# A decoder block on one core: group loads behind the fourth weight load of a group, and row fetches spread evenly

## The chip, the cores and the metric

The kernel runs on one core of a Trainium2 chip. The metric is device time in microseconds (us), shorter is better. TensorE multiplies, VectorE (DVE) and ScalarE (ACT) work elementwise, GpSimd (POOL) does elementwise work and issues indirect DMAs, and SyncE (SP) only issues DMAs.

## The reference

One hybrid decoder block for 512 tokens of width 2048 in float32: a gated mixer (an mLSTM branch and an RWKV-7 branch), then PEER, a retrieval of single-neuron experts, then an RMSNorm. The change lies in PEER:

```python
q = (xt @ w_query).reshape(NT, PEER_HEADS, 2, D_KEY // 2)
s = einsum('nhpd,pkd->nhpk', q, sub_keys)
...  # top 16 of 16 x 16 sums per head: idx [token, 128], gate = softmax(best)
act = gelu(einsum('cd,ced->ce', xc, expert_u[ic]))
out = einsum('ce,ced->cd', gc * act, expert_v[ic])
```

There are 128 x 128 = 16384 experts, each with a row of 2048 in `expert_u` and in `expert_v`; each token uses 8 heads x 16 = 128 of them.

## The kernel before, in words

PEER is done in two ways side by side. For the first 128 tokens (G) the expert rows themselves are fetched: 128 fetches of u rows, each an indirect DMA of GpSimd that brings one row of 2048 for each of the 128 tokens (1.05 MB), and then 128 fetches of v rows. VectorE uses each: a u row is multiplied with the token and summed into `dots` (line 1416), a v row is scaled by `coef` and added to a sum that lies in four PSUM banks (line 1419). Between the two halves stands one change: ScalarE's gelu of `dots`, VectorE's `coef` (lines 1462 to 1465). For the other 384 tokens (N) all experts are computed densely: 128 score units give gelu(x u) of 128 experts each, stored in `gelu_scratch`; the gates are laid out densely in `gates_scratch`; and 32 groups of 4 x 128 experts, in 4 units each (`pe_values`), multiply gate times gelu with all v rows.

All weights come through one stream of 396 units of 128 x 2048 floats (1.05 MB). SP loads unit n into `raw[n % 2]` once GpSimd has finished with unit n - 2 (`load_unit`, line 333); ScalarE copies it to a high part `wh` once TensorE has used unit n - 2 (`split_hi`, line 339); GpSimd subtracts for a low part `wl` (`split_lo`, line 343); TensorE does 48 matmuls, three for each of 16 blocks. A value group needs 1.5 MB besides: its gates `gt` and activations `act` (`load_group`, lines 514 and 515), on SP's queue among the weight loads. GpSimd multiplies them (`gated`, line 629), ScalarE makes the high half `gah`, VectorE the residual `gal` (line 1423), all one group ahead; TensorE waits for the last residual of a group before its first unit. Buffers of two groups alternate, so pass g of the loop sends group g + 2 once the residuals of group g are made (`gal_ready`). The very first pass also sends group 1, at its third load, and waits for all of `gelu_scratch` to be stored before it sends group 2.

GpSimd's program is: split of a unit, then the row fetches that stand behind it in a list, then `gated`. The list has two parts: `REST_FETCHES` for the last 40 score units (r = 0 to 39, the first fetch at r = 2) and `VALUE_FETCHES` for the 128 value units (k = 0 to 127). Before, there are two fetches behind each unit until the u rows end at k = 27, none at k = 28 to 30, and 2, 1, 2, 1, ... v rows from k = 31 to 115. A fetch waits until VectorE has used the row that had its buffer (`row_used`); there are three buffers (`ROWS_REST`) in the score part and five from two fetches into the value part. VectorE uses the rows behind unit k - 1 between its additions of unit k, after the second and the third (`dve_values`). The first u row can't be used before TensorE has transposed the 128 tokens (`xd`), which stands behind the fourth of these 40 score units.

Of the kernel before, what the change touches and what calls it, by code (L numbers as in the profile page):

```python
# [57 lines left out]
SLOTS = HEADS * TOPK  # L58
# [5 lines left out]
GROUPS = NKEYS // GE  # L64
NC4 = D // T
N_UNITS = U_PEER + NC4 * GROUPS


F_REST = NKEYS - SC_REST
REST_FETCHES = [range(2 * r - 4, 2 * r - 2) if 2 <= r < F_REST - 2 else range(0) for r in range(F_REST)]  # L70
N_REST = REST_FETCHES[F_REST - 3][-1] + 1
V_FIRST = 31
VALUE_FETCHES = [range(min(N_REST + 2 * k, SLOTS), min(N_REST + 2 * k + 2, SLOTS)) for k in range(V_FIRST)]
for k in range(V_FIRST, NC4 * GROUPS):
    at = SLOTS + 3 * ((k - V_FIRST) // 2) + 2 * ((k - V_FIRST) % 2)
    VALUE_FETCHES.append(range(min(at, 2 * SLOTS), min(at + 2 - (k - V_FIRST) % 2, 2 * SLOTS)))
assert not VALUE_FETCHES[NC4 * 7] and not VALUE_FETCHES[NC4 * 29 + 1]

ROWS_REST, ROWS = 3, 5
ROW_AT = [n % ROWS_REST if n < N_REST + 2 else n % ROWS for n in range(2 * SLOTS)]  # L80
# [3 lines left out]

R_GATED = F_REST - 5


def score_unit(e):
    return U_QUERY + PER_HEAD * (e // SC_HEAD) + 2 + e % SC_HEAD if e < SC_HEAD * HEADS else U_ROUTED + e - SC_HEAD * HEADS
# [47 lines left out]
def build(nc, stream, lora_w, params, x_t, keys_t, u_rows, v_rows, out_t):  # L137
# [13 lines left out]
    with ctx:  # L151
# [178 lines left out]
        def load_unit(sp, n, s, first=False):  # L330
            if not first:
                sp.wait_ge(w_lo, n - 1)
            sp.dma_start(raw[s][:, :], stream[bass.ds(n, 1)].rearrange("a p n -> p (a n)")).then_inc(w_loaded[s], 16)
# [7 lines left out]
        def split_lo(pool, n, s):  # L341
            pool.wait_ge(w_hi, n + 1)
            pool.tensor_tensor(wl[s][:, :], raw[s][:, :], wh[s][:, :].bitcast(F32), ALU.subtract).then_inc(w_lo, 1)  # L343
# [101 lines left out]
        def _(sp):  # L445
# [66 lines left out]
            def load_group(g, s):  # L512

                sp.dma_start(gt[s][:, :, :], gate_d[:, :, bass.ds(GE * g, GE), :].rearrange("b p e t -> p b (e t)")).then_inc(group_in[s], 16)
                sp.dma_start(act_[s][:, :, :], act_d[bass.ds(GE * g, GE)].rearrange("e p t -> p e t")).then_inc(group_in[s], 16)
# [8 lines left out]
            def load_values(g, s, ahead=True, first=False):  # L524

                for c in range(NC4):
                    load_unit(sp, U_PEER + NC4 * g + c, c % 2)
                    if c == 1 and ahead:
                        for r in range(2):
                            sp.wait_ge(pre_stored[r], 16 + 8 * NKEYS)  # L530
                        sp.wait_ge(gal_ready, GE * g + GE)
                        load_group(g + 2, s)
                    if c == 2 and first:
                        sp.wait_ge(w_used, U_PEER)
                        load_group(1, 1)

            for s in range(2):
                load_values(s, s, first=s == 0)
            with sp.Fori(1, GROUPS // 2 - 1) as i:
                for s in range(2):  # L540
                    load_values(2 * i + s, s)
            for s in range(2):
                load_values(GROUPS - 2 + s, s, ahead=False)
# [7 lines left out]
        def _(pool):  # L551
# [68 lines left out]
            def fetch(n):  # L620
                if ROW_LAST[n] is not None:
                    pool.wait_ge(row_used, ROW_LAST[n] + 1)
                pool.indirect_dma_start(rowb[ROW_AT[n]][:, :], None, u_rows if n < SLOTS else v_rows,  # L623
                                        bass.IndirectOffsetOnAxis(ap=idx[:, n % SLOTS:n % SLOTS + 1], axis=0)).then_inc(row_in[ROW_AT[n]], 16)
# [6 lines left out]

            for r in range(F_REST):
                split_lo(pool, score_unit(SC_REST) + r, r % 2)
                if r == 2:
                    pool.wait_ge(slots_ready, 1)
                    for s in range(2):
                        pool.wait_ge(gates_stored[s], 16 + 8 * GB)
                for n in REST_FETCHES[r]:
                    fetch(n)
# [4 lines left out]
            for k in range(NC4 * GROUPS):  # L644
                g, c = divmod(k, NC4)
                split_lo(pool, U_PEER + k, c % 2)
                if k == 1:
                    pool.wait_ge(w_used, U_PEER)
                for n in VALUE_FETCHES[k]:
                    fetch(n)  # L650
# [9 lines left out]
        def _(act):  # L660
# [336 lines left out]
            def act_halves(g, s, e):  # L997
                act.wait_ge(ga_ready, GE * g + e + 1)
                act.activation(gah[s][:, e, :], act_[s][:, e, :], ACT.Copy).then_inc(gah_ready, 1)  # L999

            def rest(e, s):
                act_ahead(e, s, score_unit(SC_REST) + e - SC_REST)
# [4 lines left out]
            for e in range(GE):  # L1007
                act_halves(0, 0, e)
            for r in range(R_GATED + 1, F_REST):
                rest(SC_REST + r, r % 2)  # L1010

            def act_values(g, s, ahead=AHEAD):
                for c in range(NC4):
                    n = U_PEER + NC4 * g + c
                    for e in ahead[c]:
                        act_halves(g + 1, 1 - s, e)
                    act.wait_ge(w_used, n + 1)
                    split_hi(act, n + 2, c % 2)

            for s in range(2):  # L1020
                act_values(s, s, AHEAD_1 if s == 0 else AHEAD)
            with act.Fori(1, 4) as i:
                for s in range(2):
                    act_values(2 * i + s, s)
            act.wait_ge(row_used, SLOTS)
            act.activation(gel[:, :], dots[:, :], ACT.Gelu).then_inc(gel_ready, 1)
            with act.Fori(4, GROUPS // 2 - 1) as i:
                for s in range(2):
                    act_values(2 * i + s, s)
            act.wait_ge(row_used, 2 * SLOTS)  # L1030
# [5 lines left out]
            g = GROUPS - 1  # L1036
# [22 lines left out]
        def _(dve):  # L1059
# [213 lines left out]
            at = slice(2 * MH - 2, 2 * MH)  # L1273
            dve.wait_ge(ymh_ready, 1)
            dve.tensor_tensor(yl_m[:, at, :], ymo[:, :, :], yh_m[:, at, :].bitcast(F32), ALU.subtract).then_inc(yml_ready, 1)
            for h in range(MH - 1):
                at = slice(2 * h, 2 * h + 2)
# [133 lines left out]
            def use(n):  # L1411

                b = rowb[ROW_AT[n]][:, :]
                dve.wait_ge(row_in[ROW_AT[n]], 16 * ROW_BEFORE[n] + 16)
                if n < SLOTS:
                    dve.scalar_tensor_tensor(b, b, 1.0, xg, ALU.mult, ALU.mult, accum_out=dots[:, n:n + 1]).then_inc(row_used, 1)  # L1416
                else:
                    dve.wait_ge(row_used, n)
                    dve.scalar_tensor_tensor(xg, b, coef[:, n - SLOTS:n - SLOTS + 1], xg, ALU.mult, ALU.add).then_inc(row_used, 1)  # L1419

            def dve_low(g, s, e):
                dve.wait_ge(gah_ready, GE * g + e + 1)
                dve.tensor_tensor(gal[s][:, e, :], act_[s][:, e, :], gah[s][:, e, :].bitcast(F32), ALU.subtract).then_inc(gal_ready, 1)  # L1423

            def dve_rows(g, c, dd):

                n = U_PEER + NC4 * g + c
                if dd == 3:
                    dve.wait_ge(w_used, n + 1)
                else:  # L1430
                    dve.wait_ge(out_ready, 3 * (NC4 * g + c) + dd + 1)
                at = H[:, 4 * c + dd, G:T]
                dve.tensor_tensor(at, bank(4 + dd)[:, 0:N], at, ALU.add).then_inc(out_added, 1)  # L1433

            def dve_values(g):

                for c in range(NC4):
                    k = NC4 * g + c
                    fetched = list(VALUE_FETCHES[k - 1]) if k else []
                    dve_rows(g, c, 0)  # L1440
                    dve_rows(g, c, 1)
                    for n in fetched[:1]:
                        use(n)
                    dve_rows(g, c, 2)
                    for n in fetched[1:]:
                        use(n)
                    for e in (AHEAD if g else AHEAD_1)[c]:
                        dve_low(g + 1, 1 - g % 2, e)
                    dve_rows(g, c, 3)
# [3 lines left out]
            dve.wait_ge(xg_ready, 1)  # L1453
            for r in range(F_REST):
                for n in REST_FETCHES[r]:
                    use(n)
                if r == R_GATED:
                    for e in range(GE):
                        dve_low(0, 0, e)
            for g in range(8):  # L1460
                dve_values(g)
            dve.wait_ge(row_used, SLOTS)
            dve.memset(xg, 0.0)
            dve.wait_ge(gel_ready, 1)
            step(dve.tensor_tensor(coef[:, :], gel[:, :], gate0[:, :], ALU.mult))
            for g in range(8, GROUPS - 1):
                dve_values(g)


            for b in range(4):  # L1470
                dve.wait_ge(sum_out, b + 1)
                at = H[:, 4 * b:4 * b + 4, 0:G]
# [8 lines left out]
            g = GROUPS - 1  # L1481
# [495 lines left out]
```

## Time and profile before

| | |
|---|---|
| Median of 3 runs (4293.15, 4306.17, 4307.22) | 4306.17 us |
| The profiled execution | 4302.8 us, of it span 4301.0 |
| Busy: TensorE, weight load, VectorE, ScalarE, GpSimd | 97, 87, 60, 30, 53% of the span |
| One split of a unit: ScalarE, GpSimd | 1.9, 4.6 us (means 1917, 4644 ns) |
| One load of a group, on SP | 768 KB of gates and 768 KB of activations |
| DMA over the span | 832.09 MB, 193 GB/s |
| Mean granted TensorE clock | 0.985 |

The span has three parts that matter here: score units with row fetches from about 2794 us, value units from 3138 to 4278 us, and in these the change from u to v rows near 3460 us. The DMA share is the mean busy share of the core's 16 DMA engines.

### The profile page before, as it was taken

What the parts mean: (1) busy time and instruction counts of PE and PEld (TensorE: products, weight loads), DVE (VectorE), ACT (ScalarE), POOL (GpSimd) and SP (SyncE); (2) the same over time, 40 slices, a digit from 0 to 9 for tenths busy, and PEclk for the clock granted to TensorE, in tenths of its full rate; (3) what the DMA queues carried; (4) which work ended last, traced back from release to release, by engine and by line L of the source; (5) the groups of instructions that cost most, each with busy time, mean ns of one, the idle gap of its engine ahead of it and who ended that gap; (6) DMA issues with size and microseconds to landing.
All of it is one profiled execution on the core that took longest, in us unless ns stands there. A gap on an engine that the chain in (4) does not pass through costs nothing.

```text
span 4301.0 us, 69877 instructions
## 1 busy us (share of the span) xinstructions
PE 4162.1 (97%) x27220; PEld 3743.0 (87%) x27220; DVE 2571.1 (60%) x3908; ACT 1306.7 (30%) x1265; POOL 2259.6 (53%) x866
## 2 busy tenths in 40 slices
PE   7999999999999999899999999999988999999998
PEld 5777777777788778799999999999978999999997
DVE  4344343444554542477775999745558777777775
ACT  4332322333322221233233444422222222222223
POOL 4333223233234344344445544567767778888884
PEclk9999999999999999999999999999999999999999
DMA  3222222222223442233334555499979989899983
GB/s 121 89 88 80 86 87 82 84 87 87 97 89 104 140 170 98 80 122 122 123 120 145 191 188 195 186 353 395 380 291 356 356 326 356 351 358 360 357 329 109
DMA packets 205230, 832.09 MB, mean 193 GB/s; under 512 B 15864, under 2 KB 98040, under 8 KB 120080
## 3 DMA queue, kind: packets, MB, share of 16 engines
q1 hardware_dynamic: 135024, 486.69, 31.5%
q0 software_dynamic: 36864, 268.45, 15.1%
q10 hardware_dynamic: 33184, 74.63, 4.5%
q8 instruction: 125, 2.05, 0.2%
q14 instruction: 33, 0.27, 0.0%
HBM read 760.99 MB, written 68.71 MB: 193 GB/s over the span
## 4 chain that ended last, share of the span: by engine, by line
PE 79%; issue 9%; POOL 4%; DVE 3%; DMA 3%; ACT 1%; SPq 0%; POOLq 0%; DVEq 0%; ACTq 0%
PE ps L348 17%; PE ps L350 16%; PE ps L349 16%; PE ps L1874 7%; PE ps L1875 7%; PE ps L1876 7%; POOL wl L343 4%; DMA raw<-stream 2%; PE ps L1578 2%; PE ps L1836 1%; ACT wh L339 1%; DVE rowb L1416 1%; DVE gal L1423 1%; PE ps L1730 0%; PE ps L1721 0%
## 5 line engine op out<-in xcount | busy, mean ns | idle before, releaser
L343 POOL TENSOR_TENSOR wl<-raw,wh 128x2048 fp32r<-128x2048 f32 x396 | 1839.0, 4644 | 1878.5 <-ACT wh L339 1878.0
L348 PE MATMUL ps<-xh,wh 128*128 128x384 f32 (+1 forms) x3904 | 1463.3, 375 | 43.4 <-POOL wl L343 22.2
L350 PE MATMUL ps<-xh,wl 128*128 128x384 f32 (+1 forms) x3904 | 1430.0, 366 | 0.0
L349 PE MATMUL ps<-xl,wh 128*128 128x384 f32 (+1 forms) x3904 | 1429.4, 366 | 0.0
L339 ACT ACTIVATE wh<-raw 128x2048 fp32r<-128x2048 f32 x396 | 759.0, 1917 | 1937.5 <-PE ps L350 1066.2
L348 PEld LDWEIGHTS ps<-xh,wh 128*128 128x128 f32 x3904 | 737.9, 189 | 140.4 <-issue 36.8
L350 PEld LDWEIGHTS ps<-xh,wl 128*128 128x128 f32 x3904 | 737.4, 189 | 83.4
L349 PEld LDWEIGHTS ps<-xl,wh 128*128 128x128 f32 x3904 | 738.1, 189 | 81.3 <-issue 7.7
L1874 PE MATMUL ps<-gah,wh 128*128 128x384 f32 x2048 | 699.7, 342 | 44.4 <-POOL wl L343 22.3
L1875 PE MATMUL ps<-gal,wh 128*128 128x384 f32 x2048 | 696.7, 340 | 0.0
L1876 PE MATMUL ps<-gah,wl 128*128 128x384 f32 x2048 | 696.1, 340 | 0.0
L1433 DVE TENSOR_TENSOR H<-ps,H 128x384 f32<-128x384 f32 x512 | 277.8, 553 | 320.3 <-PE ps L1876 317.5
L1874 PEld LDWEIGHTS ps<-gah,wh 128*128 128x128 f32 x2048 | 388.5, 190 | 49.5 <-issue 18.8
L1875 PEld LDWEIGHTS ps<-gal,wh 128*128 128x128 f32 x2048 | 388.7, 190 | 0.0
L1876 PEld LDWEIGHTS ps<-gah,wl 128*128 128x128 f32 x2048 | 388.5, 190 | 0.0
L1416 DVE SCALAR_TENSOR_TENSOR rowb<-rowb,ps 128x2048 f32<-128x2048 f32 x128 | 291.9, 2282 | 161.1 <-DMA rowb<-u_rows,idx 137.3
L1419 DVE SCALAR_TENSOR_TENSOR ps<-rowb,coef,ps 128x2048 f32<-128x2048 f32 x128 | 300.3, 2346 | 0.0
L623 POOL DMA_INDIRECT rowb<-u_rows,idx x128 | 123.4, 964 | 91.1 <-DVE rowb L1416 73.7
L1379 DVE TENSOR_SCALAR oh<-ps,EGT,gate_l 128x128 fp32r<-128x128 f32 x384 | 154.7, 403 | 0.0
L1379 DVE TENSOR_SCALAR oh<-ps,EGT,gate_h 128x128 fp32r<-128x128 f32 x384 | 154.7, 403 | 0.0
L1423 DVE TENSOR_TENSOR gal<-act,gah 128x384 fp32r<-128x384 f32 x128 | 150.5, 1197 | 1.4 <-ACT gah L999 1.4
L623 POOL DMA_INDIRECT rowb<-v_rows,idx x128 | 126.5, 988 | 25.7 <-issue 17.1
(321 smaller groups left out, 3700.6 us busy)
## 6 DMA issues: line engine op xcount, KB each, us to landing
raw<-stream SPq DMA_DIRECT2D x396, 1024.0 KB, 4.8
gelu_scratch<-preb ACTq DMA_DIRECT2D x128, 192.0 KB
gates_scratch<-stage ACTq DMA_DIRECT2D x12, 2048.0 KB, 6.5
gt<-gates_scratch SPq DMA_DIRECT2D x32, 768.0 KB
act<-gelu_scratch SPq DMA_DIRECT2D x32, 768.0 KB
mergegate_scratch<-sgb ACTq DMA_DIRECT2D x32, 256.0 KB, 2.1
sgm<-mergegate_scratch SPq DMA_DIRECT2D x32, 256.0 KB, 2.7
h_in<-x_t SPq DMA_DIRECT2D x4, 1024.0 KB, 8.8
```

The lines of the kernel that those rows point to most:

```text
L339: act.activation(wh[s][:, :], raw[s][:, :], ACT.Copy).then_inc(w_hi, 1)
L343: pool.tensor_tensor(wl[s][:, :], raw[s][:, :], wh[s][:, :].bitcast(F32), ALU.subtract).then_inc(w_lo, 1)
L348: pe.matmul(dst, w_h, h[:, kx, lo:], start=start, stop=False)
L349: pe.matmul(dst, w_h, l[:, kx, lo:], start=False, stop=False)
L350: return pe.matmul(dst, w_l, h[:, kx, lo:], start=False, stop=stop)
L1379: last = dve.tensor_scalar(oh1[:, 4 * c + u, m, :], iota_ps, EGT[:, 0, bass.ds(at + u, 1)], gate[:, bass.ds(at + u, 1)], ALU.is_equal, ALU ...
L1416: dve.scalar_tensor_tensor(b, b, 1.0, xg, ALU.mult, ALU.mult, accum_out=dots[:, n:n + 1]).then_inc(row_used, 1)
L1419: dve.scalar_tensor_tensor(xg, b, coef[:, n - SLOTS:n - SLOTS + 1], xg, ALU.mult, ALU.add).then_inc(row_used, 1)
L1433: dve.tensor_tensor(at, bank(4 + dd)[:, 0:N], at, ALU.add).then_inc(out_added, 1)
L1874: pe.matmul(dst, w_h, gah[s][:, e, :], start=e == 0, stop=False)
L1875: pe.matmul(dst, w_h, gal[s][:, e, :], start=False, stop=False)
L1876: last = pe.matmul(dst, w_l, gah[s][:, e, :], start=False, stop=e == GE - 1)
```

## The change

The wait for the residuals and the load of group g + 2 stand behind the fourth weight load of pass g and no longer behind the second. The row fetches are spread by rounding: 128 u rows over 74 units (r = 2 to 37 and k = 0 to 37), 128 v rows over 78 units (k = 39 to 116). The change from u to v rows, on ScalarE and VectorE, stands in front of group 10 and no longer of group 8.

```diff
+V_GROUP = 10
+U_UNITS, V_UNITS = F_REST - 4 + NC4 * V_GROUP - 2, NC4 * 29 - (NC4 * V_GROUP - 1) + 1
+even = lambda i, units: range(SLOTS * i // units, SLOTS * (i + 1) // units)
-REST_FETCHES = [range(2 * r - 4, 2 * r - 2) if 2 <= r < F_REST - 2 else range(0) for r in range(F_REST)]
+REST_FETCHES = [even(r - 2, U_UNITS) if 2 <= r < F_REST - 2 else range(0) for r in range(F_REST)]
 N_REST = REST_FETCHES[F_REST - 3][-1] + 1
-V_FIRST = 31
-VALUE_FETCHES = [range(min(N_REST + 2 * k, SLOTS), min(N_REST + 2 * k + 2, SLOTS)) for k in range(V_FIRST)]
-for k in range(V_FIRST, NC4 * GROUPS):
-    at = SLOTS + 3 * ((k - V_FIRST) // 2) + 2 * ((k - V_FIRST) % 2)
-    VALUE_FETCHES.append(range(min(at, 2 * SLOTS), min(at + 2 - (k - V_FIRST) % 2, 2 * SLOTS)))
+VALUE_FETCHES = []
+for k in range(NC4 * GROUPS):
+    i = k - (NC4 * V_GROUP - 1)
+    n = even(i, V_UNITS) if 0 <= i < V_UNITS else range(0)
+    VALUE_FETCHES.append(even(F_REST - 4 + k, U_UNITS) if k < NC4 * V_GROUP - 2 else range(SLOTS + n.start, SLOTS + n.stop))
...
                     load_unit(sp, U_PEER + NC4 * g + c, c % 2)
-                    if c == 1 and ahead:
+                    if c == 3 and ahead:
                         for r in range(2):
                             sp.wait_ge(pre_stored[r], 16 + 8 * NKEYS)
                         sp.wait_ge(gal_ready, GE * g + GE)
...
-            with act.Fori(1, 4) as i:
+            with act.Fori(1, V_GROUP // 2) as i:
...
-            with act.Fori(4, GROUPS // 2 - 1) as i:
+            with act.Fori(V_GROUP // 2, GROUPS // 2 - 1) as i:
...
-            for g in range(8):
+            for g in range(V_GROUP):
                 dve_values(g)
...
-            for g in range(8, GROUPS - 1):
+            for g in range(V_GROUP, GROUPS - 1):
                 dve_values(g)
```

The counts that result: r = 2 to 37 get 1, 2, 2, 1, 2, 2, 2, 1, ... (62 u rows in 36 units, 72 before); k = 0 to 37 get 66 u rows (2, 1, 2, 2, 1, 2, 2, 2, 1, ...); k = 38 none; k = 39 to 116 get 1, 2, 1, 2, 2, 1, 2, 2, ... v rows. The three row buffers last until fetch 63 and the five start at fetch 64 (73 and 74 before).

## Rows read from the trace of the kernel before

**Rows 1.** Sums by stretch: length, busy us (instructions) per engine, clock, DMA share, GB/s

```profile
2794.00:2833.00 39.00, 30.86 (x169) 30.58 (x168) 12.20 (x11) 6.89 (x7) 21.90 (x12) 0.87 0.74 278
2833.00:3034.00 201.00, 201.00 (x1144) 201.00 (x1144) 107.73 (x95) 55.05 (x48) 154.49 (x71) 1.00 0.99 393
3034.00:3138.00 104.00, 96.56 (x537) 95.53 (x535) 51.05 (x44) 29.17 (x28) 73.92 (x36) 0.98 0.87 340
3138.00:3206.00 68.00, 49.97 (x250) 49.02 (x251) 39.15 (x40) 9.93 (x10) 39.10 (x22) 0.85 0.86 322
3206.00:3443.00 237.00, 217.28 (x1195) 214.84 (x1195) 197.56 (x224) 59.88 (x52) 183.48 (x95) 0.97 0.88 347
3443.00:3498.00 55.00, 51.59 (x285) 51.27 (x285) 38.14 (x37) 13.58 (x12) 40.86 (x20) 0.97 0.77 298
3498.00:4242.00 744.00, 743.77 (x4228) 742.98 (x4227) 531.42 (x562) 207.31 (x180) 615.15 (x295) 1.00 0.87 337
```

**Rows 2.** DMA issues of the page: count, KB each, median us to landing

```profile
raw<-stream SPq DMA_DIRECT2D x396, 1024.0 KB, 4.8
```

**Rows 3.** Timeline beside a v group: start us, us, engine and operation, idle before

```profile
3551.21 4.63 POOL L343 TENSOR_TENSOR wl<-raw,wh 128x2048 fp32r<-128x2048 f32 x1 [0.20 <-ACT wh L339]
...
3559.53 0.38 SPq L514 DMA_DIRECT2D gt<-gates_scratch  x1
...
3575.45 1.92 ACT L339 ACTIVATE wh<-raw 128x2048 fp32r<-128x2048 f32 x1 [7.00 <-DMA raw<-stream]
```

**Rows 4.** Timeline beside a u group: GpSimd's split, ScalarE's split two units later

```profile
3371.95 4.63 POOL L343 TENSOR_TENSOR wl<-raw,wh 128x2048 fp32r<-128x2048 f32 x1
...
3400.37 1.92 ACT L339 ACTIVATE wh<-raw 128x2048 fp32r<-128x2048 f32 x1 [11.97 <-DMA raw<-stream]
```

**Rows 5.** Timeline of ScalarE, VectorE and GpSimd where row fetches begin

```profile
2803.63 1.92 ACT L339 ACTIVATE wh<-raw 128x2048 fp32r<-128x2048 f32 x1 [6.17 <-PE ps L350]
...
2813.67 2.29 DVE L1416 SCALAR_TENSOR_TENSOR rowb<-rowb,ps 128x2048 f32<-128x2048 f32 x1 [23.57 <-PE ps L1855]
...
2816.24 0.94 POOL L623 DMA_INDIRECT rowb<-u_rows,idx  x1 [13.33 <-DVE rowb L1416]
2817.19 4.52 POOL L343 TENSOR_TENSOR wl<-raw,wh 128x2048 fp32r<-128x2048 f32 x1
```

**Rows 6.** Timeline: load of group 0 and ScalarE's split of the load behind it

```profile
3034.74 0.39 SPq L514 DMA_DIRECT2D gt<-gates_scratch  x1
...
3058.50 1.92 ACT L339 ACTIVATE wh<-raw 128x2048 fp32r<-128x2048 f32 x1 [12.02 <-DMA raw<-stream]
```

**Rows 7.** Sums of a stretch behind a stall, columns as in rows 1

```profile
3250.20:3257.00 6.80, 5.19 (x16) 5.20 (x17) 3.38 (x4) 2.40 (x2) 6.33 (x5) 0.50 0.60 225
```

**Rows 8.** Timeline of the first value units: GpSimd, SP, ScalarE, VectorE

```profile
3129.36 4.62 POOL L343 TENSOR_TENSOR wl<-raw,wh 128x2048 fp32r<-128x2048 f32 x1 [3.82 <-ACT wh L339]
...
3146.25 2.37 SPq L333 DMA_DIRECT2D raw<-stream  x1
...
3156.39 1.91 ACT L339 ACTIVATE wh<-raw 128x2048 fp32r<-128x2048 f32 x1 [18.28 <-DMA raw<-stream]
...
3175.20 6.57 DVE L1423 TENSOR_TENSOR gal<-act,gah 128x384 fp32r<-128x384 f32 x2
```

**Rows 9.** Waits from 3134 to 3206 us: in total, times, longest us

```profile
PE ps L1874 <- DVE gal L1423: 8.3, 1, 8.3
...
PE ps L1874 <- POOL wl L343: 7.5, 1, 7.5
```

**Rows 10.** SP's waits for residuals, 3206 to 3443 us, then 3498 to 4242 us

```profile
SPq L514 <- DVE gal L1423: 24.5, 6, 10.4
...
SPq L514 <- DVE gal L1423: 56.8, 20, 3.1
```

**Rows 11.** Costliest groups of the page: busy us, mean ns of one, idle before

```profile
L1416 DVE SCALAR_TENSOR_TENSOR rowb<-rowb,ps 128x2048 f32<-128x2048 f32 x128 | 291.9, 2282 | 161.1 <-DMA rowb<-u_rows,idx 137.3
```

**Rows 12.** Timeline of VectorE at the change from u to v rows

```profile
3462.21 4.25 DVE L1465 TENSOR_TENSOR coef<-gel,gate 128x128 f32<-128x128 f32 x1
```

More of the change, by code:

```diff
@@ L69 @@
 F_REST = NKEYS - SC_REST
-REST_FETCHES = [range(2 * r - 4, 2 * r - 2) if 2 <= r < F_REST - 2 else range(0) for r in range(F_REST)]
+V_GROUP = 10
+U_UNITS, V_UNITS = F_REST - 4 + NC4 * V_GROUP - 2, NC4 * 29 - (NC4 * V_GROUP - 1) + 1
+even = lambda i, units: range(SLOTS * i // units, SLOTS * (i + 1) // units)
+REST_FETCHES = [even(r - 2, U_UNITS) if 2 <= r < F_REST - 2 else range(0) for r in range(F_REST)]
 N_REST = REST_FETCHES[F_REST - 3][-1] + 1
-V_FIRST = 31
-VALUE_FETCHES = [range(min(N_REST + 2 * k, SLOTS), min(N_REST + 2 * k + 2, SLOTS)) for k in range(V_FIRST)]
-for k in range(V_FIRST, NC4 * GROUPS):
-    at = SLOTS + 3 * ((k - V_FIRST) // 2) + 2 * ((k - V_FIRST) % 2)
-    VALUE_FETCHES.append(range(min(at, 2 * SLOTS), min(at + 2 - (k - V_FIRST) % 2, 2 * SLOTS)))
-assert not VALUE_FETCHES[NC4 * 7] and not VALUE_FETCHES[NC4 * 29 + 1]
+VALUE_FETCHES = []
[3 more added lines that the diff above has]
+    VALUE_FETCHES.append(even(F_REST - 4 + k, U_UNITS) if k < NC4 * V_GROUP - 2 else range(SLOTS + n.start, SLOTS + n.stop))
+assert sum(map(len, REST_FETCHES + VALUE_FETCHES)) == 2 * SLOTS and not VALUE_FETCHES[NC4 * 29 + 1]
 ROWS_REST, ROWS = 3, 5
```

## The prediction

> **What bounds the kernel now.** I read the per-stretch sums first [rows 1]. TensorE is the bound wherever nothing stands in its way: in the stretch 3498 to 4242 us it did 4228 matmuls in 744.0 us, 5.68 per us, so a unit of 48 matmuls takes 8.44 us. With 5.69 per us as the full rate, each stretch's loss is its length less its matmuls over 5.69:
> - 2794 to 2833 (first row fetches): 39.0 - 169/5.69 = 9.3 us
> - 2833 to 3034 (score units with two fetches each): 201.0 - 1144/5.69 = 0
> - 3034 to 3138: 104.0 - 537/5.69 = 9.6
> - 3138 to 3206 (first value units): 68.0 - 250/5.69 = 24.1
> - 3206 to 3443 (rest of the u rows): 237.0 - 1195/5.69 = 27.0
> - 3443 to 3498 (change to v rows): 55.0 - 285/5.69 = 4.9
> - 3498 to 4242 (v rows): 744.0 - 4228/5.69 = 0.9
>
> Together 75.8 us, all that a new order of transfers and rows can win. Where TensorE did not lose, the DMA is nearly full: 393 GB/s at share 0.99, with no matmul lost. So saturation alone costs nothing; what costs is a weight transfer that stands behind a group's 1.5 MB. In the 201 us stretch weight transfers (1.05 MB) land in about 4.8 us, the page's median [rows 2], in spite of two rows of 1.05 MB each.
>
> **The deadline of a weight transfer.** Call t = 0 the end of the low split of unit n-2, when SP may send the load of unit n. ScalarE splits unit n when TensorE ends unit n-2, 10.2 us later in steady state; the two splits (1.9 and 4.6 us) end 1.4 us before TensorE needs them. A load issued right behind a group therefore follows 8.4 us after the preceding one, and must have landed 8.4 + 10.2 + 1.4 = 20.0 us after the split that let the preceding one go. In a v group [rows 3] that split ended at 3551.21 + 4.63 = 3555.84, the group went at 3559.53 and its follower landed at 3575.45: 19.6 us, 0.4 to spare. In the seventh u group [rows 4] the split ended at 3371.95 + 4.63 = 3376.58, landing 3400.37: 23.8 us, 3.8 late. Between them lie three bursts of rows (2, 1, 2) against (2, 2, 2); one more row of 1.05 MB at 393 GB/s is 2.7 us.
>
> **Part 1, a later start of the rows.** Before, fetches 2 and 3 follow the third split of that stage; row 3 needs row 0's buffer, and row 0 can't be used before TensorE has transposed xd, behind the unit that precedes. GpSimd stands for 13.33 us in front of the fetch and its split starts at 2817.19 though ScalarE's half began at 2803.63 and took 1.9 [rows 5]. With the even spread the counts for r = 2, 3, 4 are 1, 2, 2: row 3 comes one split later, so the split at 2817.19 goes back to about 2805.5 and TensorE runs that unit straight after the transposes, at 2813.5. Then GpSimd waits for rows 0 and 1 (done at 2815.9 and 2818.1), its next split ends at 2819.3 + 4.6 = 2823.9, and TensorE, free at 2821.9, waits 2.0 us. Loss 9.3 becomes 2.0: -7.3. Bounds: 0 (the stall moves on whole) to -9.3.
>
> **Part 2, group 0.** It goes at 3034.74, and its follower lands at 3058.50 [rows 6], 23.8 us behind it where the v group's came 15.9 behind and had 0.4 to spare. TensorE's stall of some 4.5 us and the half clock behind it are 6.0 of the 9.6 lost. The clock's part: after such a stall the granted clock was 0.50 (1.2 GHz of 2.4), and 5.19 us of busy TensorE held 16 matmuls, worth 2.8 at the full rate: 2.4 us for the longest, 1.5 for shorter ones [rows 7]. In the new plan score units carry 62/36 = 1.72 rows, (1.72 + 1) x 1.05 + 0.20 for the gelu store = 3.05 MB in 8.44 us, 361 GB/s instead of 396, and the bursts there are (2, 2, 1). I take 2 us late, no half clock: -4 (0 to -6).
>
> **Part 3, the first value groups.** SP stands behind the last gelu store before it sends group 2, and the raw load of value unit 2 behind it goes only at 3146.25, 12.3 us after its buffer was free; ScalarE gets it at 3156.39 [rows 8]. Behind the fourth load, group 2 no longer blocks units 2 and 3; group 1 goes at once after load 2. Unit 2 then lands by 3140 and costs nothing (TensorE waits 7.5 us for it before). Next in line is the residual of group 1, for which TensorE waits 8.3 us [rows 9]. It came late because two of VectorE's subtractions took 6.57 us [rows 8] where GpSimd's split lay beside them. New: rows 64 to 66 are taken in bursts 1, 2, 2; row 65 shares its buffer with row 63 across the change from three to five buffers, so GpSimd stands some 3 us once. I get the split of unit 3 at 3160.8 to 3165.4, the last residual of group 1 at 3176, against 3172 wanted: 4 us late, 1 for the clock. Loss 24.1 becomes 5: -19. Bounds: -5 (the residuals are as late as before) to -22.
>
> **Part 4, u groups.** Value units carry 66/38 = 1.74 u rows instead of 2: 3.26 MB a unit, 387 GB/s for 419. 419 can't be had, 387 just can. SP's wait for the residual (24.5 us in six waits, up to 10.4 [rows 10]) goes: behind the fourth load that semaphore is long reached. But a wait shorter than 4.8 us cost nothing, since the weight load ahead still occupied the same queue; only the one or two long ones did. Queued behind the moved group are load 0 of the next group and nothing else that waits: its data are wanted by GpSimd 25 us later. VectorE was busy 197.6 us for 24.9 units [rows 1], 7.9 each, and slipped at times; 0.26 row less of 2.28 us [rows 11] makes it 7.3 of 8.44. By the pass g of the loop that sends a group, the bursts beside it are (2, 2, 2) in passes 1 and 2, (2, 2, 1) in 3 to 5, and in the others (2, 1, 2) or less. Late by 2.4 + 0.8 for two, by 1.5 for three: 11; 3 more for VectorE, and 4 for the change to v rows, where coef's 4.25 us beside GpSimd's split stays [rows 12] and one row fewer is fetched. 31.9 becomes 18: -14. Bounds: +5 to -28.
>
> **Part 5, v groups.** 128 rows now go over 78 units instead of 85: 1.64 a unit, 3.16 MB, 375 GB/s for 357. Six of the 20 passes (11, 13, 18, 20, 25, 27) get (2, 2, 1). They land at 19.6 to 19.6 + 2.7 = 22.3, say 21.5: 1.5 late, 9 us; 3 for the others, which have 0.4 to spare. SP's 56.8 us there [rows 10], at most 3.1 each, are no gain, by the 4.8 above. +12. Bounds: 0 to 20 x (3.8 + 1.5) = +106.
>
> **Sum.** 4302.8 us (span 4301.0 and 1.8 around it) - 7.3 - 4 - 19 - 14 + 12 = 4270.5, 4271. The profiled execution is 3.4 below the median of the runs; I leave that.
>
> **A rule against it.** [rows 1] has 393 GB/s over 201 us, more than any stretch of the new plan asks for. The Trainium skill, "DMA: Bandwidth & Descriptors", section Specifications, gives about 358 GB/s as the HBM limit of a core. With that limit the v stretch would be full already and the sum would be rival B's; the trace disagrees by the 393.
>
> **Rivals.**
> - A, v groups starve (slower). A group gives way to rows on other queues; with a (2, 2, 1) burst or 7 rows in a pass (most of the 20) a backlog builds, and all followers come 3.8 late with 1.5 for the clock: 4258.5 (the sum without part 5) + 106 = 4364. It decides from (4302.8 - 4258.5)/20 = 2.2 us a group. For: 0.4 us to spare. Against: u groups with 8 rows lost only 27/7 = 3.9 each, VectorE's share included.
> - B, a transfer limit near what the v stretch asks for now, 357: groups of 12.65 MB take 35.4 for 33.8 us, 19.5 x 1.6 = 31, and 12 more in the u groups: 4258.5 + 31 + 12 = 4302, no change. Against: the 393.
> - C, with rows even and loads apart no follower is late: 4302.8 - 7.3 - 6 - 19 - 28 = 4242. For: TensorE lost nothing at 393 GB/s, and no u group is as full as before. Against: the bursts (2, 2, 2) stay in two groups.
> - D, part 3 only shifts the stall from load 2 to the residuals: -5 instead of -19, 4285.
>
> **Chances.** Forecast 0.55 (its own range 4255 to 4284), C 0.16, D 0.15, B 0.07, A 0.07. Range 4243 to 4297: it takes in C's edge and D, leaves out A and half of B. What can be told from no change is 0.3%, 13 us, from the median 4306.2: faster 0.86, same 0.07, slower 0.07.
>
> **What would show it.** Part 1: no GpSimd wait of over 5 us for a row near 2803, and the split of that unit near 2805. Part 2: the load behind group 0 within 22 us. Part 3: the load of value unit 2 issued near 3134 less the shift, no TensorE wait for it, under 5 us for the residual. Parts 4 and 5: SP's wait for residuals gone; late followers in the (2, 2, ...) groups only, granted clock mostly 1.00 from the third group on, 370 to 378 GB/s in the v stretch. Half-clock stretches scattered over the v groups, or followers beyond 20 us in (2, 1, 2) groups, would prove it wrong.

## The result and the profile after

Median 4315.62 us (4310.69 to 4325.36, 8 runs) against 4301.20 (8 runs): ratio 1.0037 [1.0023, 1.0051]. The change made the kernel 0.4% slower; forecast was 4271, range 4243 to 4297. The profiled execution took 4310.7 (span 4309.0 and 1.7 around it), 7.9 more than the one before; the medians are 14.4 apart.

Sums by stretch of the kernel after, with the borders and columns of [rows 1]:

```profile
2794.00:2833.00 39.00, 37.02 (x217) 36.66 (x217) 12.24 (x11) 10.45 (x9) 25.84 (x12) 1.00 0.84 317
2833.00:3034.00 201.00, 201.00 (x1147) 201.00 (x1146) 95.47 (x84) 53.80 (x49) 149.88 (x65) 1.00 0.92 363
3034.00:3138.00 104.00, 96.71 (x524) 95.92 (x523) 40.88 (x37) 26.93 (x26) 69.95 (x31) 0.95 0.84 322
3138.00:3206.00 68.00, 58.23 (x321) 57.58 (x321) 48.06 (x55) 17.28 (x15) 48.96 (x26) 0.95 0.85 324
3206.00:3443.00 237.00, 223.23 (x1247) 220.07 (x1246) 192.58 (x217) 62.50 (x53) 190.95 (x99) 0.99 0.90 353
3443.00:3498.00 55.00, 47.43 (x241) 46.16 (x240) 51.51 (x47) 11.76 (x10) 36.41 (x18) 0.91 0.80 313
3498.00:4242.00 744.00, 721.54 (x4058) 716.75 (x4057) 581.10 (x557) 200.44 (x173) 601.51 (x297) 0.99 0.87 341
```

The loss of each (length less matmuls over 5.69), against the same from [rows 1]:

| stretch | before | forecast for after | after |
|---|---|---|---|
| 2794 to 2833 | 9.3 | 2.0 | 0.9 |
| 3034 to 3138 | 9.6 | 5.6 | 11.9 |
| 3138 to 3206 | 24.1 | 5 | 11.6 |
| 3206 to 3498 | 31.9 | 18 | 17.8 + 12.6 = 30.4 |
| 3498 to 4242 | 0.9 | 12.9 | 30.8 |

The borders stand still while the work moves by up to 20 us, so these sums are good to a few us. The starts of single units by the trace give the same picture: value unit 48 starts at 3585.7 (before 3599.5), 13.8 us ahead; the last matmul of the value units starts at 4286.8 (before 4278.2), 8.6 behind. In 80 units of the v rows 22.4 us went.

Who waits in the v stretch, 3498 to 4242, in total us, times and longest; first the kernel after:

```profile
ACT wh L343 <- DMA raw<-stream: 49.8, 7, 7.5
PEld ps L1878 <- DVE H L1437: 26.6, 13, 2.3
PE ps L1878 <- DVE H L1437: 22.5, 13, 2.0
```

and the same wait of ScalarE in the kernel before, which in that stretch has no wait of TensorE on VectorE at all:

```profile
ACT wh L339 <- DMA raw<-stream: 140.5, 20, 7.9
```

ScalarE waits for a transfer 7 times instead of 20. That is no sign of faster transfers: with the group in its new place and TensorE at its full pace (e5 below) it waits 20 times again, 139.3 us. What moved is the place. Before, all 20 waits stand in the second unit of a pass, where the gates and the first residual of the next group lie; in e5 they stand in the fourth. TensorE, in turn, now waits 13 times for H, which is VectorE adding TensorE's results and so freeing their PSUM bank, and never for a split or for weights. VectorE's own groups in that stretch, before and then after (busy us, mean ns of one), show what holds it:

```profile
L1423 DVE TENSOR_TENSOR gal<-act,gah 128x384 fp32r<-128x384 f32 x88 | 82.3, 954 | 0.0
```

```profile
L1427 DVE TENSOR_TENSOR gal<-act,gah 128x384 fp32r<-128x384 f32 x85 | 117.0, 1396 | 0.0
```

The same subtraction, the residual that I named in part 3, takes half as long again on average. One by one they lie near a few values: in the v passes 0.55 us, about 1.9, 5.0 or 6.5. Here is one and the same place in the kernel before and after: VectorE has used two v rows in the unit and comes to the first residual. Timeline of the kernel before, ScalarE, VectorE and GpSimd (start us, us, engine and operation, idle before it):

```profile
3541.66 1.99 POOL L629 TENSOR_TENSOR act<-act,gt 128x384 f32<-128x384 f32 x2
3541.89 2.19 DVE L1423 TENSOR_TENSOR gal<-act,gah 128x384 fp32r<-128x384 f32 x1
3542.07 1.92 ACT L339 ACTIVATE wh<-raw 128x2048 fp32r<-128x2048 f32 x1 [7.09 <-DMA raw<-stream]
...
3544.00 1.48 DVE L1433 TENSOR_TENSOR H<-ps,H 128x384 f32<-128x384 f32 x3
3544.07 4.63 POOL L343 TENSOR_TENSOR wl<-raw,wh 128x2048 fp32r<-128x2048 f32 x1 [0.41 <-ACT wh L339]
```

and of the kernel after:

```profile
3557.01 1.93 ACT L343 ACTIVATE wh<-raw 128x2048 fp32r<-128x2048 f32 x1 [6.12 <-PE ps L1880]
...
3557.59 2.01 POOL L633 TENSOR_TENSOR act<-act,gt 128x384 f32<-128x384 f32 x2
3558.10 6.47 DVE L1427 TENSOR_TENSOR gal<-act,gah 128x384 fp32r<-128x384 f32 x1
3559.53 4.61 POOL L347 TENSOR_TENSOR wl<-raw,wh 128x2048 fp32r<-128x2048 f32 x1
...
3564.49 1.47 DVE L1437 TENSOR_TENSOR H<-ps,H 128x384 f32<-128x384 f32 x3
```

Both residuals start while GpSimd multiplies two gates. Before, GpSimd then stands 0.41 us, because ScalarE's half of the split came late, and it came late because its weights did (7.09 us of waiting for the transfer behind the group). The gates end at 3543.65 and the residual 0.43 us later (3544.08), when that gap closes. After, the weights of this unit are there, ScalarE starts 0.6 us ahead of the gates instead of 0.4 behind, GpSimd goes from the gates into its split without a gap, and the residual ends at 3564.57, when the split is over (3564.14). Three additions have queued up behind it, TensorE has no free bank.

Theory L is that: a residual on VectorE (both inputs in SBUF) stands until GpSimd's elementwise operation beside it is over, and as a rule also over the next one if that follows without a gap; the late transfer had been a hold that made the gap. The margin was thin. In the 20 v passes of the kernel before, the gap at this place was 0.1 to 1.2 us in 17; in passes 14, 18 and 20 the trace shows none (0.02 us or less), and there the residual still came through first and the split took 0.3 us longer, as here in pass 20:

```profile
3879.60 1.98 DVE L1423 TENSOR_TENSOR gal<-act,gah 128x384 fp32r<-128x384 f32 x1
3881.11 4.97 POOL L343 TENSOR_TENSOR wl<-raw,wh 128x2048 fp32r<-128x2048 f32 x1
```

In the kernel after it costs 2.0 to 3.8 us in each of the seven v passes in whose units VectorE uses 2,1,2,... rows. Pass 16 has the same rows as every v pass of the kernel before (2,1,2,1) and still loses 2.3 where nothing was lost, its residual 6.54 us for 1.97. The rival is R, late followers: the v groups of the bursts (2,2,...) delay the load behind them, as part 5 had it. In the v stretch of the kernel after no wait of TensorE speaks for it.

On the lock itself the Trainium skill, "SBUF — State Buffer", section "SBUF: two separate sides", says that VectorE and GpSimd share a port pair under an exclusive lock, which a VectorE operation with two SBUF inputs takes too against a GpSimd operation that reads SBUF, and that who starts first has it for the whole instruction. The trace agrees: 0.55 us alone, 6.47 beside the split. What the trace adds is that the waiting residual mostly did not get its turn between two GpSimd instructions that followed without a gap: so it was in all of e1's passes 9 to 28 below (6.4 to 6.7 us). The residual came first in the three passes just named and in pass 15 of the kernel after. No run gave the residual an operand in PSUM; that it is this lock and no other bond between the two engines rests on the page and on the durations.

### The profile page after: what moved, and what is told of

Same layout as the page of the kernel before. It is cut to its first block, busy times and chain, and to the rows that moved or that the text cites. A ratio compares the mean times of both kernels' runs of the same rounds, so it can differ in the third digit from the quotient of the medians.

```text
span 4309.0 us, 69877 instructions
## 1 busy us (share of the span) xinstructions
PE 4164.2 (97%) x27220; PEld 3739.7 (87%) x27220; DVE 2618.6 (61%) x3908; ACT 1310.0 (30%) x1265; POOL 2259.8 (52%) x866
## 4 chain that ended last, share of the span: by engine, by line
PE 76%; issue 10%; DVE 7%; POOL 4%; DMA 2%; ACT 1%; POOLq 0%; SPq 0%; DVEq 0%; ACTq 0%
PE ps L352 17%; PE ps L354 16%; PE ps L353 16%; PE ps L1878 6%; PE ps L1879 6%; PE ps L1880 6%; POOL wl L347 4%; DVE gal L1427 2%; PE ps L1582 2%; DVE ps L1423 1%; DMA raw<-stream 1%; DVE rowb L1420 1%; PE ps L1840 1%; DVE H L1437 1%; ACT wh L343 1%
## 5 line engine op out<-in xcount | busy, mean ns | idle before, releaser
L1427 DVE TENSOR_TENSOR gal<-act,gah 128x384 fp32r<-128x384 f32 x128 | 200.3, 1586 | 4.2 <-ACT gah L1003 4.2
L627 POOL DMA_INDIRECT rowb<-v_rows,idx x128 | 125.1, 977 | 27.0 <-issue 21.2
```

## The experiments

All compute the full result. Each comparison is with the kernel before on the same chip: medians 4304.19 (17 runs) for the first four, 4305.71 (11) for the next four, 4306.88 (11) for the last three.

**e1, the move alone** (kernel before):

```diff
-                    if c == 1 and ahead:
+                    if c == 3 and ahead:
```

> Rows as before, only the group load behind the fourth weight load. Theory L (lock): in the changed kernel every v pass with rows 2, 1, 2, x at its four units lost 2.0 to 3.8 us at its second unit, where the residual beside it took 6.5 us; in the kernel before the same rows 2, 1, 2, 1 lost nothing because the weight load behind the group came late and held GpSimd's next split back until the residual was through. With the group moved and the rows 2, 1, 2, 1 in all of 19 v passes, each then loses some 2.5 us: v stretch about 45 us longer than before, first residual 6.5 us in each pass; start of the value units 12 us shorter; total about 4301 + 45 - 12 = 4334. Rival R (rows: the loss comes from more v rows per unit and from transfers behind the group): v stretch as before, total about 4301 - 15 = 4286.

Measured 4377.6 (4374.5 to 4379.8), ratio 1.017 [1.0151, 1.0189]: 73 us slower with no transfer more and no row moved. The v stretch (borders as in [rows 1]), the residuals in it, and TensorE's waits:

```profile
3498.00:4242.00 744.00, 704.83 (x3804) 698.41 (x3803) 583.21 (x516) 186.55 (x159) 562.77 (x278) 0.95 0.83 321
```

```profile
L1423 DVE TENSOR_TENSOR gal<-act,gah 128x384 fp32r<-128x384 f32 x80 | 161.2, 2034 | 0.0
```

```profile
PE ps L1874 <- DVE H L1433: 39.2, 20, 2.2
```

20 waits, one in each v pass, none for weights: 744 - 3804/5.69 = 75.5 us lost where it was 0.9. The waits are 39.2 of it; the granted clock of 0.95 over the stretch, 1.00 in [rows 1], is the other half (0.05 x 744 = 37, an estimate). Here every v pass is (2,1,2,1), so all meet the lock; in the kernel after only seven begin so. The sign was expected, the size was not (4334 expected): each of passes 9 to 28 loses 3.7 to 4.0 us, the clock included, for 2.5 in the expectation.

**e2, the rows alone** (kernel after, the group back behind the second load):

```diff
-                    if c == 3 and ahead:
+                    if c == 1 and ahead:
```

> Rows spread as in the change, the group load behind the second weight load as before. Theory L: passes with rows 2, 1, 2, x keep the hold and lose nothing to the lock, v stretch within 10 us of before; 8 us are won where the rows begin; total 4285 to 4295. Rival R: the v passes lose what they lose in the changed kernel (about 22 us), the start of the value units 24 us as before, total about 4315 to 4325.

Measured 4304.55 (10 runs), 0.9997 [0.9983, 1.001]: nothing, between both expectations. The (2,1,2,...) passes lose less, as L has it: the first residual takes 1.9 to 2.0 us in six of seven, and four of them lose nothing, two 0.7 and 1.1, pass 11 (6.44 us) 2.2. But passes 15, 17, 22 and 24 with rows (2,2,1,2), all but one without loss in the kernel after, now lose 1.9 to 4.3 without a long residual: the load behind the group reaches ScalarE 22.1 to 22.7 us behind the split that let its predecessor go. There R's mechanism is right, with two rows in a row beside the group. So neither half alone gives what both give: 0 and +73 alone, +14 together (4315.6 against 4301.2). Of the twenty v passes that meet the lock when only the group is moved, seven still meet it in full when the rows are spread too, and passes 10, 15, 26 and 28 in another residual (5.0 us).

**e3 and e11, the residual ahead of the second row** (kernel after; VectorE's order in a unit):

```diff
                     dve_rows(g, c, 2)
-                    for n in fetched[1:]:
-                        use(n)
                     for e in (AHEAD if g else AHEAD_1)[c]:
                         dve_low(g + 1, 1 - g % 2, e)
+                    for n in fetched[1:]:
+                        use(n)
                     dve_rows(g, c, 3)
```

> The changed kernel, but VectorE makes the residuals ahead of the second row of a unit, so 2.3 us earlier, before GpSimd's gates and its next split; the same operations in number. Theory L: no residual of a v pass takes over 2.5 us, v stretch back to what the matmuls take (22 us less), u passes some 10 less, start 3 less: total 4275 to 4285. Rival R: nothing changes, 4315.

> The changed kernel with residuals ahead of the second row, in more rounds and beside the two others: 4263.

Measured 4263.32 (4260.3 to 4269.9), 0.9908 [0.9888, 0.9928], and again 4264.1, 0.9902 [0.9877, 0.9926]. No work and no transfer is changed, the residual only comes 2.7 us earlier, before GpSimd's gates. The same place in the timeline, and the v stretch:

```profile
3542.89 0.98 POOL L627 DMA_INDIRECT rowb<-v_rows,idx  x1 [0.16 <-issue]
3542.91 0.58 DVE L1427 TENSOR_TENSOR gal<-act,gah 128x384 fp32r<-128x384 f32 x1
```

```profile
3498.00:4242.00 744.00, 734.90 (x4158) 729.82 (x4158) 535.16 (x583) 219.31 (x195) 598.22 (x291) 1.00 0.86 335
```

```profile
L1427 DVE TENSOR_TENSOR gal<-act,gah 128x384 fp32r<-128x384 f32 x84 | 58.4, 715 | 0.0
```

715 ns a residual instead of 1396; 52 us below the kernel after, more than the 30 to 40 expected; the first value groups and the u groups are freed too: 237.0 - 1306/5.69 = 7.5 lost in 3206 to 3443 (17.8), 3138 to 3206 3.5 (11.6). In the v stretch 13.2 is left: by units, 1.1 in pass 11, 1.9 in 13 and 0.6 in 25 are late followers in (2,2,...) bursts (in e11's trace 2.3 in 13, 0.7 in 20 and 2.2 in 27); the value units now end at 4235.7, so 6.3 more is other work inside the fixed border.

**e4, a hold on GpSimd** (kernel after; GpSimd waits behind the gates until the first residual of the next group is made):

```diff
                     for e in (AHEAD if g else AHEAD_1)[c]:
                         gated(g + 1, 1 - g % 2, e)
+                    if g and c == 1:
+                        pool.wait_ge(gal_ready, GE * (g + 1) + 1)
```

> The changed kernel, but behind the gates of each pass's second unit GpSimd waits for the first residual of the next group before it starts the next split. Theory L: first residuals take about 2 us for 6.5, the split starts up to 1.5 us late and ends in time, v stretch 15 to 22 us less, total 4290 to 4300. Rival R: the added wait can only cost, 4315 or more.

Measured 4285.24 (8 runs), 0.9952 [0.9936, 0.9969]: 30 us below the kernel after. In the (2,1,2,...) v passes the first residuals are at 1.8 to 2.0 us; some later ones, which the added wait does not guard, are caught instead (pairs of 5.9 to 6.6 us in six v passes, where an undisturbed pair takes 1.0). The gain is more than the 15 to 25 expected.

**e5, the same hold on e1:**

> The kernel with only the group load moved, and GpSimd waits behind the gates of each pass's second unit for the first residual of the next group. Theory L: the added wait does what the late weight load did before, all 19 v passes with rows 2, 1, 2, 1 lose nothing again, first residual near 2.0 us for 6.5, v stretch some 60 us shorter than without the wait: about 4377 - 60 - 10 = 4307. Rival R: a wait can't win, 4377.

Measured 4292.2, 0.9972 [0.996, 0.9983]. The v stretch, its residuals, ScalarE's waits for weights and the added wait:

```profile
3498.00:4242.00 744.00, 744.00 (x4235) 743.70 (x4235) 532.97 (x568) 211.03 (x184) 610.10 (x292) 1.00 0.86 337
```

```profile
L1425 DVE TENSOR_TENSOR gal<-act,gah 128x384 fp32r<-128x384 f32 x88 | 83.8, 971 | 0.0
```

```profile
ACT wh L339 <- DMA raw<-stream: 139.3, 20, 7.4
...
POOL wl L343 <- DVE gal L1425: 10.1, 20, 0.5
```

This is the sharpest pair: e1 and e5 differ by one added wait, which can only delay GpSimd and in the v stretch does so by 0.5 us a pass. It takes 85 us off (15 more than expected) and brings TensorE in the v stretch from 3804 matmuls to 4235, the residual from 2034 ns to the 971 that it was before (954). A rival in which the move hurts through transfers, SP's queue or a shortage of buffers would have left e1's loss as it was; ScalarE's waits for weights are no shorter than before the change (140.5 us in 20).

**e6, residual first on e1, and e7, on the kernel before** (the edit of e3):

> Rows as before, group load moved, residuals ahead of the second row. Theory L: v stretch at the matmuls' pace as before, u passes (eight rows each) lose only late followers, start of the value units 15 us better than before: 4270 to 4280. Rival R: 4377. Against the spread with the same order (4263) it shows what the spread is worth once the lock is out of the way: 8 us where the rows begin, and the u passes.

> The kernel before, with residuals ahead of the second row and nothing else. Theory L: the u passes lose the second half of their losses (what comes behind a late split stays, 4 to 5 us a pass in four passes), the v passes nothing: 4285 to 4295, and the 24 us at the start of the value units hardly change, since there SP stands behind the last store. Rival R: 4303.

Measured 4275.1, 0.9925 [0.9908, 0.9941], and 4285.76, 0.9953 [0.9938, 0.9969]. With the lock out of the way the three steps stand side by side (medians; the kernel before was measured four times, once with each set of runs):

| | residual last | residual first |
|---|---|---|
| kernel before | 4301.2, 4304.2, 4305.7, 4306.9 | 4285.8 |
| group moved (e1, e6) | 4377.6 | 4275.1 |
| group moved and rows spread (after; e3, e11) | 4315.6 | 4263.3, 4264.1 |

In the right column the move brings 11 us and the spread another 11 to 12; in the left the same edits bring +73 and then -62. The forecast reasoned in the right column and the chip ran the left; even in the right one both edits together bring 22 us, where 32 were forecast. e6 loses 3.1 to 3.5 at the fourth unit of u passes 1 to 3, the late followers of (2,2,2) bursts that part 4 had.

**e8 and e10, the bursts apart** (on e3; the rows of a pass are 2, 2, 1, 2, so that the three bursts beside a group are 2, 1, 2):

```diff
-VALUE_FETCHES = []
+VALUE_FETCHES, at = [], N_REST
 for k in range(NC4 * GROUPS):
-    i = k - (NC4 * V_GROUP - 1)
-    n = even(i, V_UNITS) if 0 <= i < V_UNITS else range(0)
-    VALUE_FETCHES.append(even(F_REST - 4 + k, U_UNITS) if k < NC4 * V_GROUP - 2 else range(SLOTS + n.start, SLOTS + n.stop))
+    n = (2, 2, 1, 2)[k % NC4] - (k == 1) if k < NC4 * V_GROUP - 2 else 0 if k == NC4 * V_GROUP - 2 else \
+        1 if k == NC4 * V_GROUP - 1 else (2, 2, 1, 2)[k % NC4]
+    n = min(n, 2 * SLOTS - at)
+    VALUE_FETCHES.append(range(at, at + n))
+    at += n
...
```

> The changed kernel with residuals ahead of the second row, and seven rows a pass placed 2, 2, 1, 2, so that the three bursts beside each group are 2, 1, 2 everywhere. The late followers of the passes with bursts 2, 2, x (losses of 1 to 4.5 us at the fourth unit of passes 2, 5, 11, 13, 25) go: 8 us below the version with the even spread, about 4255. If the followers were not late for the bursts, the same 4263.

> The version with bursts 2, 1, 2 beside every value group, in more rounds: 4258, 5 us below the version with the even spread, as in the first measurement.

Measured 4258.52, 0.9892 [0.9875, 0.9908], and 4256.91, 0.9885 [0.9861, 0.9909]: 7.2 us below e11 on the same chip, 4.8 below e3 on another. The expectation was 8 below e3. The late followers go with the (2,2,...) bursts: in e8 none of passes 11 to 28 loses more than 0.8, in e10 one does (1.7 at the fourth unit of pass 23). That holds though 7 rows go in nearly every pass instead of 6 or 7: in these runs it counts how the rows lie beside the group.

**e9, the same beside group 0** (on e8; two score units' counts swapped from 2, 1 to 1, 2):

```diff
+REST_FETCHES[30], REST_FETCHES[31] = (lambda at: (range(at, at + 1), range(at + 1, at + 3)))(REST_FETCHES[30].start)
```

> The version with bursts 2, 1, 2 beside every value group, and the same done beside group 0: bursts 2, 2, 1 in the score units there become 2, 1, 2. The load behind group 0 landed 25 us after the split before it; if the burst decides, it lands near 22 and 3 to 5 us go: 4 us below the next version. If the small packets of the group and the gelu stores decide, nothing changes.

Measured 4252.02 (4245.0 to 4255.3), 0.9868 [0.9843, 0.9892], 4.9 below e10 (4252.2 to 4261.1; the ranges overlap). ScalarE's split of the load behind group 0, in the kernel after, in e10 and in e9:

```profile
3048.79 1.92 ACT L343 ACTIVATE wh<-raw 128x2048 fp32r<-128x2048 f32 x1 [12.54 <-DMA raw<-stream]
```

```profile
3047.66 1.92 ACT L346 ACTIVATE wh<-raw 128x2048 fp32r<-128x2048 f32 x1 [12.71 <-DMA raw<-stream]
```

```profile
3044.99 1.92 ACT L348 ACTIVATE wh<-raw 128x2048 fp32r<-128x2048 f32 x1 [8.08 <-DMA raw<-stream]
```

That is 25.1, 25.3 and 20.6 us behind the end of GpSimd's split that let the preceding load go. The stretch 3034 to 3138 loses 104.0 - 559/5.69 = 5.8 in e9, 104.0 - 526/5.69 = 11.6 in e10, 11.9 in the kernel after. This version beats both kernels, by 1.3% and 1.5%.

## Why the prediction was wrong

**Where it failed.** The step is the one under "The deadline of a weight transfer", used again in parts 4 and 5: that a transfer behind a group can only cost by coming late, so that to take the group out of the way of units 2 and 3 is worth 0 or more. Part 5 put nothing for what else that would start earlier, and the runs showed some 30 us for it in the kernel after and 75 with the move alone (e1). I had both facts that contradict it. [rows 8] shows two subtractions at 6.57 us beside GpSimd's split, and part 3 even names the cause. I used it for one place, put "3 more for VectorE" for the u passes, and nothing for the 20 v passes. And [rows 3] shows in one v group that ScalarE's split comes late by the transfer; it is so in all 20 (140.5 us of its waiting). The question not asked was what else starts earlier when they don't wait, and whom it meets. Part 4's "7.3 of 8.44" is a sum of busy time; with 1.1 us to spare in a unit it says nothing of an operation that turns from 0.55 to 6.5 us by a shift of half a microsecond. None of the rivals A to D had this mechanism. A had the sign and the stretch, by another cause: e1 has no wait of TensorE for weights in the v stretch, and e5 wins the loss back without touching a transfer.

**Part 1, right.** -7.3 forecast, -8.4 measured. GpSimd's split begins at 2804.43 (forecast about 2805), and its longest wait for a row is 5.97 us for 13.33:

```profile
2804.43 4.62 POOL L347 TENSOR_TENSOR wl<-raw,wh 128x2048 fp32r<-128x2048 f32 x1 [1.45 <-ACT wh L343]
2815.03 0.96 POOL L627 DMA_INDIRECT rowb<-u_rows,idx  x1 [5.97 <-DVE rowb L1420]
```

It is a little over the 5 us that I had set as the mark.

**Part 2, wrong.** Loss 11.9 for 9.6, forecast 5.6. The mean rate in the score units fell as reckoned (363 GB/s for 393 in 2833 to 3034), but the follower came 25.1 us behind the split that let its predecessor go (24.6 before, beside bursts 2,2,2), where I had taken 22 ("2 us late") from the mean and the burst (2,2,1). e9 keeps the mean and only puts the single row between the double ones: 20.6. It then loses 5.8, the forecast's size by a means that the change doesn't have.

**Part 3, half.** The load of value unit 2 goes without waiting and nothing stands for it, as forecast. GpSimd stands 3.2 us once for a row, also as forecast, and TensorE 1.9 us for the split behind it. The residual behind it costs more than "4 us late": one wait of 7.9 us, where 8.3 stood in [rows 9]:

```profile
PE ps L1878 <- DVE gal L1427: 7.9, 1, 7.9
```

```profile
3154.71 3.75 DVE L1427 TENSOR_TENSOR gal<-act,gah 128x384 fp32r<-128x384 f32 x2
...
3167.51 6.69 DVE L1427 TENSOR_TENSOR gal<-act,gah 128x384 fp32r<-128x384 f32 x2
```

Rival D is what happened, in half: 24.1 to 11.6, for 5. e3 puts it at 3.5, so the 8 us between go with the residuals' place.

**Part 4, wrong in size.** 31.9 stayed 30.4. SP's wait for residuals went, as forecast, and the followers of passes 2, 3 and 4 came 22.6, 21.9 and 21.7 us behind the split and cost 4.0 together. But passes 7 to 9, which carried the change and v rows before, now have three double u rows, their first residuals take 6.6 to 7.5 us, and they lose 6.6, 7.1 and 5.9. Passes 8 and 9 fill the stretch 3443 to 3498, which loses 12.6 for 4.9; the change itself now lies behind it, near 3510. In e3 the same stretches lose 7.5 + (55.0 - 311/5.69) = 7.8: then -24, more than my -14.

**Part 5, wrong by what it left out, and too dear in what it reckoned.** The followers of passes 11, 13, 18, 20, 25 and 27 were to come 21.5 us behind the split and to cost 9 us. In the kernel after only those of 25 and 27 made ScalarE wait (22.2 and 22.1 us), at no cost to TensorE. In the other four ScalarE waited for TensorE, held back by the lock, so its start tells nothing of the transfer; e1 has the same 22.4 in its passes with bursts 2,1,2. With the lock gone (e3) the six followers come at 21.2, 22.2, 20.1, 19.5, 20.7 and 19.1 us and cost 1.1, 1.9 and 0.6 in 11, 13 and 25 and nothing in the others: 4 us, not 9. The +29.9 measured is the lock: seven passes with 2.0 to 3.8, 20.1 together, and 11.0 in passes 10, 15, 26 and 28, where one residual took 5.0 (by units; the fixed borders give 1 less).

**The marks.** "Granted clock mostly 1.00 from the third group on" and "370 to 378 GB/s in the v stretch" failed: the clock was 0.98 to 1.00 and the rate 361 GB/s in 3560 to 3960, where TensorE waited; e3 has 374 and 373 there.

## What to carry to other kernels

Before you make a transfer or an engine earlier, look at what its lateness holds back: list what will start earlier, and find in the trace any operation with two very different durations (here 0.55 and 6.5 us) that could now fall beside it. Sums of busy time per unit don't show that; the spread of one line's durations does. When two edits interact, measure them in a square: a step that costs 73 us in one order was worth 11 in the other. In these runs the bursts beside a large transfer counted by their order (2,1,2 or 2,2,1) where the mean was the same (e9 against e10).

## What the hardware showed that was not expected

- A VectorE subtraction of two SBUF tiles (128x384) took 0.55 us alone, 1.9 to 2.2 when it began beside GpSimd's two gates and GpSimd then stood 0.1 us or more, and 6.3 to 6.7 in the v passes when GpSimd went from the gates to the split without a gap. The bond goes both ways: GpSimd's split took 4.5 to 4.7 us in most value units and up to 5.0 where a residual was still under way at its start (4.97 at 3881.11 in the kernel before). Products and sums with an operand in PSUM kept 2.3 and 0.55 us throughout.
- One added wait on GpSimd made the program 85 us faster (e5 against e1); one transfer group sent two loads later made it 73 slower (e1).
- The load behind a 1.5 MB group landed 20.6 or 25.3 us after the split ahead of it (e9, e10), by whether one row of 1.05 MB lay between the double ones or behind them. With a double row in its place it was 24.6 (kernel before).
